# Products of 128 stationary columns in a chunked RWKV recurrence, with one PSUM bank per row side and copies split between ScalarE and VectorE

## The chip, the core and the metric

The kernel runs on one core of one Trainium2 chip. The metric is the device time of the whole program in microseconds, from inputs in HBM to the output in HBM. It is one launch of straight-line code on five engines (TensorE, VectorE, ScalarE, GpSimd, SyncE) that meet through semaphores.

## What is computed

One layer of a diffusion backbone over 2048 latent tokens with 256 context tokens: a token mixer with retention and a bidirectional RWKV-7 scan, then an expert-choice mixture of experts. The change touches only the RWKV scan:

```python
def step(s, xt):                       # per head, 64 x 64 state, every token
    wt, kt, vt, kkt, at = xt[:5]
    sa = jnp.einsum('bhvk,bhk->bhv', s, -kkt)
    s = (s * wt[:, :, None, :] + sa[..., None] * (kkt * at)[:, :, None, :]
         + vt[..., None] * kt[:, :, None, :])
    return s, jnp.einsum('bhvk,bhk->bhv', s, xt[5])
...
for d, f in enumerate((_ident, _flip)):      # both directions, 8 heads
    s_state, o = _rwkv7_scan(zero_rw, f(st_c['w'][d]), f(st_c['k'][d]), f(st_c['v']), f(st_c['kk']), f(st_c['a'][d]), None)
    _, o = _rwkv7_scan(s_state, f(st_l['w'][d]), f(st_l['k'][d]), f(st_l['v']), f(st_l['kk']), f(st_l['a'][d]), f(qu_l['r']))
```

(Cut and joined from the reference.) Everything is float32.

## The kernel before

Stages follow one another: a projection, the scan (`rwkv_chunks`, lines 147 to 876), retention, the mix of heads, the router and the experts. The scan runs the tokens in chunks of 128 per direction, 18 tiles times two directions: 36 slabs, the directions by turns (j % 2). A slab is two halves t of 64 tokens, and eight heads. Inside a half the recurrence is a triangular system, so a slab needs:

- **The inverse.** `pairs` makes the masked products of keys and decayed queries; `couple(l)` and `double(l)` for l from 0 to 4 build the inverse by doubling in f16. VectorE masks what couple made (`levels`, Xb); ScalarE copies what double made (`copies`, Tb and TTb). `errors` and `refine` then sharpen it in f32 (Er, ErH, Gr).
- **The recurrence of a half**, in a chain: `values` (keys' block times v) and `from_state` (decayed keys times the state Hb) add up the right side and, in another part of the bank, the output; ScalarE copies the right side to R (`right_side`); `solve` multiplies by the inverse Gr; ScalarE copies the solution to U (`solved`); `state` makes the new state, which VectorE adds and decays (H, Hb); `outputs` adds U's part of the output, and ScalarE copies it to yo.

Partitions hold two sides of 64 rows, `side(0)` below and `side(1)` above. Each product of 64x64 uses one quarter of the array, and the two sides run beside each other. Half t has a PSUM bank PB[t]: columns 0 to 255 hold the right side and then the solution, 256 to 511 the output. AR holds kkn (k=0) and r (k=1), scaled; BK holds per head four blocks of 64 columns, of which 2 and 3 go into `values`. PB[0] is also RB[1], where the refinement works.

Every engine runs its own list in a fixed order, written out by hand in one loop over the step h. In step h slab h is inverted, slab h+1 is prepared (VectorE's `running`, `centred` D, `exclusive` D2, beta, kappa; ScalarE's exponentials e_bk, e_al, e_rho; GpSimd's products into AR), half 0 of slab h-1 and half 1 of slab h-2 are solved. So pieces of the recurrence stand between the dependent products of the inverse. e_bk waits for D2 (semaphore dd2). SP loads three slabs ahead and stores yo; its waits on `yc` and on the loads' buffers stay.

`pe.matmul(out, stationary, moving)`: the profile's row names the moving operand first and gives stationary rows*columns, then rows x moving columns. One f32 call is two matmul records with two weight loads, one f16 call is one of each.

## Time and profile before

| | us |
|---|---|
| median of 3 runs | 4031.0 (4029.63 to 4033.84) |
| the profiled execution | 4023.1 |
| its span | 4021.3 |
| TensorE matmuls busy in it | 3634.7 (90%) |
| VectorE, ScalarE busy | 2190.9 (54%), 1844.0 (46%) |
| the scan's first and last copy of R | 1297.9, 2131.7 |

The span is the time from the first to the last instruction of the core in one profiled execution; rows carry times from its start. A matmul's end is modelled, and matmuls overlap, so the start of the next is the better measure of pace. "PEld" is the weight load. An idle time "<-issue" is one in which the engine waited for nothing that the profile shows. A group's row in a timeline covers its instructions from the first start to the last end.

### The profile page before, as it was taken

What the parts mean: (1) busy time and instruction counts of PE and PEld (TensorE: products, weight loads), DVE (VectorE), ACT (ScalarE), POOL (GpSimd) and SP (SyncE); (2) the same over time, 40 slices, a digit from 0 to 9 for tenths busy, and PEclk for the clock granted to TensorE, in tenths of its full rate; (3) what the DMA queues carried; (4) which work ended last, traced back from release to release, by engine and by line L of the source; (5) the groups of instructions that cost most, each with busy time, mean ns of one, the idle gap of its engine ahead of it and who ended that gap; (6) DMA issues with size and microseconds to landing.
All of it is one profiled execution on the core that took longest, in us unless ns stands there. A gap on an engine that the chain in (4) does not pass through costs nothing. (4 is left out here: it accounts for less than half of the span.)

```text
span 4021.3 us, 93358 instructions
## 1 busy us (share of the span) xinstructions
PE 3634.7 (90%) x39394; PEld 3022.9 (75%) x39394; DVE 2190.9 (54%) x3518; ACT 1844.0 (46%) x2997; POOL 708.5 (18%) x901
## 2 busy tenths in 40 slices
PE   7999999999997888888787889995799999999993
PEld 6777877878786777777776767784688888888883
DVE  4553453553444666666666864456445445444545
ACT  5653543543443555555555453332344444444443
POOL 1111010010112223232221343100011111111110
PEclk9999999999998999999999999997899999999996
DMA  7566566564556443444414476654466666666667
GB/s 259 187 221 211 166 207 188 153 199 142 172 176 146 100 93 90 91 98 98 111 44 127 152 226 212 200 172 181 145 204 216 219 219 201 217 216 216 205 211 300
DMA packets 443709, 702.90 MB, mean 175 GB/s; under 512 B 182488, under 2 KB 321344, under 8 KB 425808
## 3 DMA queue, kind: packets, MB, share of 16 engines
q1 hardware_dynamic: 409504, 587.23, 47.1%
q0 software_dynamic: 33840, 110.40, 9.0%
q8 instruction: 278, 4.55, 0.5%
q14 instruction: 87, 0.71, 0.1%
HBM read 531.97 MB, written 165.56 MB: 173 GB/s over the span
## 5 line engine op out<-in xcount | busy, mean ns | idle before, releaser
L113 PE MATMUL fro__acc<-fro__hT_hi,fro__wh 128*128 128x512 f32 (+1 forms) x1608 | 629.4, 391 | 12.6 <-DVE fro__hT_lo L2684 8.9
L114 PE MATMUL fro__acc<-fro__hT_hi,fro__wl 128*128 128x512 f32 (+1 forms) x1608 | 614.8, 382 | 0.0
L115 PE MATMUL fro__acc<-fro__hT_lo,fro__wh 128*128 128x512 f32 (+1 forms) x1608 | 614.4, 382 | 0.0
L2014 DVE TENSOR_TENSOR fin__wl<-fin__raw,fin__wh 128x4096 fp32r<-128x4096 f32 x96 | 424.7, 4424 | 317.1 <-ACT fin__wh L1958 317.1
L2690 DVE TENSOR_TENSOR fro__wl<-prj__w,fro__wh 128x1024 fp32r<-128x1024 f32 x201 | 246.3, 1225 | 584.9 <-ACT fro__wh L2427 584.6
L1958 ACT ACTIVATE fin__wh<-fin__raw 128x4096 fp32r<-128x4096 f32 x96 | 348.4, 3629 | 191.2 <-PE exp__acc L115 190.3
L113 PE MATMUL exp__acc<-fin__wh,exp__xh 128*128 128x512 f32 x1024 | 399.9, 390 | 0.7 <-DVE exp__xl L2019 0.7
L115 PE MATMUL exp__acc<-fin__wl,exp__xh 128*128 128x512 f32 x1024 | 398.5, 389 | 0.0
L114 PE MATMUL exp__acc<-fin__wh,exp__xl 128*128 128x512 f32 x1024 | 398.5, 389 | 0.0
L113 PEld LDWEIGHTS fro__acc<-fro__hT_hi,fro__wh 128*128 128x128 f32 x1608 | 305.1, 190 | 87.3 <-issue 31.3
L115 PEld LDWEIGHTS fro__acc<-fro__hT_lo,fro__wh 128*128 128x128 f32 x1608 | 304.9, 190 | 59.2
L114 PEld LDWEIGHTS fro__acc<-fro__hT_hi,fro__wl 128*128 128x128 f32 x1608 | 305.3, 190 | 57.4 <-issue 2.6
L2437 ACT ACTIVATE fro__pool<-fro__acc 128x512 f32<-128x512 f32 (+1 forms) x136 | 79.6, 586 | 433.6 <-PE fro__acc L115 417.8
L566 DVE TENSOR_TENSOR rwc__Xb<-rwc__XB,rwc__level 128x256 f16<-128x256 f32 x360 | 137.1, 418 | 171.6 <-PE rwc__XB L705 169.6
L113 PEld LDWEIGHTS exp__acc<-fin__wh,exp__xh 128*128 128x128 f32 x1024 | 192.3, 188 | 40.4 <-DVE exp__xl L2019 1.1
L115 PEld LDWEIGHTS exp__acc<-fin__wl,exp__xh 128*128 128x128 f32 x1024 | 192.2, 188 | 40.0
L114 PEld LDWEIGHTS exp__acc<-fin__wh,exp__xl 128*128 128x128 f32 x1024 | 192.3, 188 | 39.3
L2427 ACT ACTIVATE fro__wh<-prj__w 128x1024 fp32r<-128x1024 f32 x201 | 212.0, 1055 | 3.5 <-DVE fro__keep L2787 3.5
L113 PE MATMUL exp__acc<-fin__wh,exp__hh 128*128 128x512 f32 x512 | 203.7, 398 | 0.0
L115 PE MATMUL exp__acc<-fin__wl,exp__hh 128*128 128x512 f32 x512 | 200.0, 391 | 0.0
L114 PE MATMUL exp__acc<-fin__wh,exp__hl 128*128 128x512 f32 x512 | 199.7, 390 | 0.0
L372 ACT ACTIVATE rwc__Tb<-rwc__TP 128x256 f16<-128x256 f32 x360 | 121.0, 387 | 69.3 <-PE rwc__TP L715 67.4
(465 smaller groups left out, 7383.3 us busy)
## 6 DMA issues: line engine op xcount, KB each, us to landing
fin__raw<-in_w_x SPq DMA_DIRECT2D x96, 2048.0 KB, 8.4
prj__w<-in_w_z SPq DMA_DIRECT2D x201, 512.0 KB, 4.2
s_zT<-fro__pool SPq DMA_DIRECT2D x128, 256.0 KB, 4.6
fro__wm<-in_w_mod POOLq DMA_DIRECT2D x16, 1024.0 KB, 6.2
mix__gate<-s_zT SPq DMA_DIRECT2D x64, 256.0 KB, 4.2
rwc__ways<-s_ways SPq DMA_DIRECT2D x36, 384.0 KB, 4.5
rwc__ways<-s_ways SPq DMA_DIRECT2D x72, 192.0 KB, 4.8
rwc__both<-s_both SPq DMA_DIRECT2D x36, 384.0 KB, 4.4
```

The costliest lines, as they stand in the source:

```text
L113: pe.matmul(out, sh, mh, start=first, stop=False)
L114: pe.matmul(out, sl, mh, start=False, stop=False)
L115: return pe.matmul(out, sh, ml, start=False, stop=last)
L372: cp = lambda out, in_, n: act.activation(out, in_, ACT.Copy).then_inc(S[n], 1)
L566: tt(Xb[:, g, :, :], h4(XB[g]), level[:, j % 2, l, None, :].to_broadcast([P, GH, HC]), ALU.mult).then_inc(S["xd"], 1)
L1958: act.activation(wh[s][:, :, :], raw[s][:, :, :], ACT.Copy).then_inc(w_hi, 1)
L2014: ve.tensor_tensor(wl[s][:, :, :], raw[s][:, :, :], wh[s][:, :, :], ALU.subtract).then_inc(w_lo, 1)
L2427: act.activation(wh[s % 3][:, :, :], w[s % 3][:, :, :], ACT.Copy).then_inc(split_hi, 1)
L2437: act.activation(zo[i % 3][:, 0:n], acc[t % 3][:, 0:n], fn).then_inc(kept, 1)
L2690: ve.tensor_tensor(wl[s % 3][:, :, :], w[s % 3][:, :, :], wh[s % 3][:, :, :], ALU.subtract).then_inc(split_lo, 1)
```

## The change

`values` and `from_state` take the two blocks of a row side in one product: 64 rows and 128 stationary columns, so the right side comes out on partitions 0 to 63 and the output on 64 to 127. Each row side x writes its own bank QB[x], which holds both halves t in 256 columns each. AR's layout follows. `solve` writes the lower partitions of both banks, `outputs` the upper. ScalarE copies the lower side's R and U, VectorE the upper side's, with semaphores rhd and ud of their own; the output takes two activations. The refinement's second part shares QB[1], so `values` of half 1 waits for Gr of the slab after it. The loops of TensorE, ScalarE and VectorE get another order.

```diff
-        AR = [sb(f"AR{u}", [P, 4, 2, C]) for u in range(B)]
+        AR = [sb(f"AR{u}", [P, 4, 2, 2, HC]) for u in range(B)]
...
-        PB = [room.ps(f"PB{t}", [P, 512]) for t in range(2)]
-        MB, RB = (XB, TP), (EB, PB[0])
+        QB = [room.ps(f"QB{x}", [P, 2, 256]) for x in range(2)]
+        MB, RB = (XB, TP), (EB[:, 0:256], QB[1][:, 0, :])
...
-        part = lambda k, q: slice(256 * k + WD * q, 256 * k + WD * q + WD)
+        part = lambda q: slice(WD * q, WD * q + WD)
...
-                gp.tensor_tensor(AR[j % B][:, :, 0, :], ld[j % LB]["kkn"][:, :, :], e_al[:, :, :], ALU.mult).then_inc(S["al"], 1)
+                gp.tensor_tensor(AR[j % B][:, :, :, 0, :], halves(ld[j % LB]["kkn"]), halves(e_al), ALU.mult).then_inc(S["al"], 1)
...
             def right_side(j, t):
                 act.wait_ge(S[f"rhm{t}"], at(f"rhm{t}", j))
-                cp(R[t][:, :], PB[t][:, 0:256], f"rhc{t}")
+                act.activation(R[t][side(0), :], QB[0][side(0), t, :], ACT.Copy).then_inc(S[f"rhc{t}"], 1)
...
             def solved(j, t):
                 act.wait_ge(S[f"uum{t}"], at(f"uum{t}", j))
-                cp(U[t][:, :], PB[t][:, 0:256], f"uc{t}")
+                act.activation(U[t][side(0), :], QB[0][side(0), t, :], ACT.Copy).then_inc(S[f"uc{t}"], 1)
...
-                cp(yo[t][:, :], PB[t][:, 256:512], f"yc{t}")
+                for x in range(2):
+                    last = act.activation(yo[t][side(x), :], QB[x][side(1), t, :], ACT.Copy)
+                last.then_inc(S[f"yc{t}"], 1)
...
                 n, inverting, prepare = h + 1, h < SLABS, h + 1 < SLABS
-                if exists(h - 2):
-                    right_side(h - 2, 1)
                 if inverting:
                     copies(1, h)
                 if exists(h - 2):
-                    solved(h - 2, 1)
+                    right_side(h - 2, 1)
                 if prepare:
                     scale_bk(n)
+                if exists(h - 2):
+                    solved(h - 2, 1)
                 if inverting:
                     copies(2, h)
+                if exists(h - 2):
+                    outputs(h - 2, 1)
                 if prepare:
                     scale_al(n)
+                if inverting:
+                    copies(3, h)
                 if exists(h - 1):
                     right_side(h - 1, 0)
-                if inverting:
-                    copies(3, h)
                 if prepare:
                     scale_rho(n)
-                if exists(h - 2):
-                    outputs(h - 2, 1)
                 if exists(h - 1):
                     solved(h - 1, 0)
                 if inverting:
@@ -568,7 +571,7 @@
...
+            def right_side(j, t):
+                ve.wait_ge(S[f"rhm{t}"], at(f"rhm{t}", j))
+                ve.tensor_copy(R[t][side(1), :], QB[1][side(0), t, :]).then_inc(S[f"rhd{t}"], 1)
+
+            def solved(j, t):
+                ve.wait_ge(S[f"uum{t}"], at(f"uum{t}", j))
+                ve.tensor_copy(U[t][side(1), :], QB[1][side(0), t, :]).then_inc(S[f"ud{t}"], 1)
...
@@ -607,8 +617,12 @@
                     refine(1, h - 1, 1)
                 if prepare:
                     centred(n)
+                if exists(h - 2):
+                    right_side(h - 2, 1)
                 if inverting:
                     levels(1, h)
+                if exists(h - 2):
+                    solved(h - 2, 1)
                 if prepare:
                     exclusive(n)
                 if inverting:
@@ -617,8 +631,12 @@
                     state(h - 2, 1)
                 if prepare:
                     scaled_removal(n)
+                if exists(h - 1):
+                    right_side(h - 1, 0)
                 if inverting:
                     levels(3, h)
+                if exists(h - 1):
+                    solved(h - 1, 0)
                 if prepare:
                     scaled_keys(n)
...
             def values(j, t):
                 u, s = j % B, turn_of(j, t)
-                if t == 0:
+                if t:
+                    pe.wait_ge(S["yc0"], at("yc0", j))
+                    if exists(j + 1):
+                        pe.wait_ge(S["gd"], at("gd", j + 1))
+                else:
                     pe.wait_ge(S["gd"], at("gd", j))
-                elif j:
-                    pe.wait_ge(S["yc1"], at("yc1", j - 1))
+                    if j:
+                        pe.wait_ge(S["yc1"], at("yc1", j - 1))
...
                 for q in range(4):
-                    for k in range(2):
-                        for x in range(2):
-                            r = side(x)
-                            m = mm(PB[t][r, part(k, q)], BK[u][r, 2 * q + s, 2 + k, :], v_t[u][r, head(q, x ^ s)], start=(q == 0 and k == 0), stop=False,
-                                   skip_group_check=True)
+                    for x in range(2):
+                        r = side(x)
+                        m = mm(QB[x][:, t, part(q)], BK[u][r, 2 * q + s, 2:4, :].rearrange("p k c -> p (k c)"), v_t[u][r, head(q, x ^ s)],
+                               start=q == 0, stop=False, skip_group_check=True)
                 m.then_inc(S[f"vm{t}"], 1)
...
                 for q in range(4):
-                    for k in range(2):
-                        for e in range(2):
-                            m = mm(PB[t][side(e ^ s), part(k, q)], AR[u][side(e), q, k, side(e ^ s)], Hb[j % 2][side(e), q, :], start=False, stop=False,
-                                   skip_group_check=True)
+                    for e in range(2):
+                        m = mm(QB[e ^ s][:, t, part(q)], AR[u][side(e), q, e ^ s, :, :].rearrange("p k c -> p (k c)"), Hb[j % 2][side(e), q, :],
+                               start=False, stop=False, skip_group_check=True)
                 m.then_inc(S[f"rhm{t}"], 1)
...
                 pe.wait_ge(S[f"rhc{t}"], at(f"rhc{t}", j))
+                pe.wait_ge(S[f"rhd{t}"], at(f"rhd{t}", j))
                 pe.wait_ge(S["gd"], at("gd", j))
                 for q in range(4):
                     n = 2 * q + s
-                    for r in map(side, range(2)):
-                        m = mm(PB[t][r, part(0, q)], Gr[j % 2][r, n // GH, n % GH, :], R[t][r, part(0, q)], start=False, stop=True, skip_group_check=True)
+                    for x, r in enumerate(map(side, range(2))):
+                        m = mm(QB[x][side(0), t, part(q)], Gr[j % 2][r, n // GH, n % GH, :], R[t][r, part(q)], start=False, stop=True, skip_group_check=True)
                 m.then_inc(S[f"uum{t}"], 1)
...
                 pe.wait_ge(S[f"uc{t}"], at(f"uc{t}", j))
+                pe.wait_ge(S[f"ud{t}"], at(f"ud{t}", j))
                 for q in range(4):
-                    for r in map(side, range(2)):
-                        m = mm(PB[t][r, part(1, q)], BK[u][r, 2 * q + s, 1, :], U[t][r, part(0, q)], start=False, stop=True, skip_group_check=True)
+                    for x, r in enumerate(map(side, range(2))):
+                        m = mm(QB[x][side(1), t, part(q)], BK[u][r, 2 * q + s, 1, :], U[t][r, part(q)], start=False, stop=True, skip_group_check=True)
...
             inverse_seed(0)
             for h in range(SLABS + 2):
                 p, n, inverting, prepare = h - 1, h + 1, h < SLABS, h + 1 < SLABS
-                if exists(h - 2):
-                    values(h - 2, 1)
-                    from_state(h - 2, 1)
                 if inverting:
                     couple(0, h)
                 if exists(p):
@@ -825,23 +845,25 @@
                 if inverting:
                     double(0, h)
                 if exists(h - 2):
+                    values(h - 2, 1)
+                    from_state(h - 2, 1)
+                if inverting:
+                    couple(1, h)
+                if exists(h - 2):
                     solve(h - 2, 1)
                 if inverting:
-                    couple(1, h)
-                if exists(p):
-                    values(p, 0)
+                    double(1, h)
+                if exists(h - 2):
+                    outputs(h - 2, 1)
                 if inverting:
-                    double(1, h)
+                    couple(2, h)
                 if exists(h - 2) and exists(h):
                     state(h - 2, 1)
                 if inverting:
-                    couple(2, h)
+                    double(2, h)
                 if exists(p):
+                    values(p, 0)
                     from_state(p, 0)
-                if inverting:
-                    double(2, h)
-                if exists(h - 2):
-                    outputs(h - 2, 1)
                 if inverting:
                     couple(3, h)
                 if exists(p):
```

Further, h4 becomes rb4 where RB is read, `state` waits for ud too, and `part` loses an argument there.

On TensorE the head of a step, before:

```order
L681 MATMUL rwc__XB<-rwc__bon,rwc__ones 32x128 x3
L756 MATMUL rwc__PB<-rwc__v_t,rwc__BK 64x64 [waits rwc__yc1]
L756 MATMUL rwc__PB<-rwc__v_t,rwc__BK 64x64 x15
L771 MATMUL rwc__PB<-rwc__Hb,rwc__AR 64x64 [waits rwc__vm1,rwc__hup0]
L771 MATMUL rwc__PB<-rwc__Hb,rwc__AR 64x64 x15
L705 MATMUL rwc__XB<-rwc__Tb,rwc__ATb 64x64 [waits rwc__tbc,rwc__trc,rwc__bonc]
```

and with the change, up to and behind the first double (L733, L738) and from there to outputs (L827):

```order
L699 MATMUL rwc__XB<-rwc__bon,rwc__ones 32x128 x3
L723 MATMUL rwc__XB<-rwc__Tb,rwc__ATb 64x64 [waits rwc__tbc,rwc__trc,rwc__bonc]
...
L738 MATMUL rwc__TTP<-rwc__TTb,rwc__Xb 64x64 x8
L777 MATMUL rwc__QB<-rwc__v_t,rwc__BK 128x64 [waits rwc__gd,rwc__yc0]
L777 MATMUL rwc__QB<-rwc__v_t,rwc__BK 128x64 x7
L791 MATMUL rwc__QB<-rwc__Hb,rwc__AR 128x64 [waits rwc__vm1,rwc__hup0]
L791 MATMUL rwc__QB<-rwc__Hb,rwc__AR 128x64 x7
L723 MATMUL rwc__XB<-rwc__Tb,rwc__ATb 64x64 [waits rwc__tbc]
...
L803 MATMUL rwc__QB<-rwc__R,rwc__Gr 64x64 [waits rwc__gd,rwc__rhd1,rwc__rhc1]
...
L827 MATMUL rwc__QB<-rwc__U,rwc__BK 64x64 [waits rwc__ud1,rwc__uc1]
```

Values and from_state no longer stand between the bonus product and couple; one couple is left between from_state and solve, one double between solve and outputs.

On ScalarE the same stretch of a step (R1, U1 belong to half 1 of slab h-2; e_bk to slab h+1; the copy of U with what stands around it), before:

```order
L372 ACTIVATE rwc__TTb<-rwc__TTP 128x512 [waits rwc__ttm]
L372 ACTIVATE rwc__U1<-rwc__PB1 128x256 [waits rwc__uum1]
L383 ACTIVATE rwc__e_bk<-rwc__D2 128x512 [waits rwc__kappad,rwc__dd2]
L372 ACTIVATE rwc__Tb<-rwc__TP0 128x256 [waits rwc__tm]
L372 ACTIVATE rwc__Tb<-rwc__TP1 128x256 [waits rwc__tm]
```

and with the change:

```order
L373 ACTIVATE rwc__TTb<-rwc__TTP 128x512 [waits rwc__ttm]
L436 ACTIVATE rwc__R1<-rwc__QB0 64x256 [waits rwc__rhm1]
L384 ACTIVATE rwc__e_bk<-rwc__D2 128x512 [waits rwc__kappad,rwc__dd2]
L440 ACTIVATE rwc__U1<-rwc__QB0 64x256 [waits rwc__uum1]
L373 ACTIVATE rwc__Tb<-rwc__TP0 128x256 [waits rwc__tm]
```

The exponential e_bk has moved ahead of the copy of U.

On VectorE (D is `centred`, L537 `exclusive`, with the semaphore dd2), with the change:

```order
L533 TENSOR_TENSOR rwc__D<-rwc__L 128x512 [waits rwc__erho,rwc__eal,rwc__dld,rwc__ebk,rwc__scan]
L596 COPY rwc__R<-rwc__QB 64x256 [waits rwc__rhm1]
L569 TENSOR_TENSOR rwc__Xb<-rwc__XB,rwc__level 128x256 [waits rwc__xm] x2
L600 COPY rwc__U<-rwc__QB 64x256 [waits rwc__uum1]
L537 TENSOR_TENSOR rwc__D<-rwc__D,rwc__ways 128x512 [waits rwc__dd]
L569 TENSOR_TENSOR rwc__Xb<-rwc__XB,rwc__level 128x256 [waits rwc__xm] x2
```

Before, the same rows stand there without the two copies. D2 now stands behind the copy of U.

## Rows read from the trace of the kernel before

**Rows 1.** Busy time by stretch, the middle of the recurrence stage, all engines.

```profile
core 0: us, PE busy (x) PEld busy (x) DVE busy (x) ACT busy (x) POOL busy (x), PEclk, DMA share, GB/s
1300.00:2110.00 810.00, 680.41 (x22994) 613.02 (x22990) 546.29 (x1181) 432.01 (x1114) 241.78 (x401) 0.99 0.40 91
```

**Rows 2.** The copying line of ScalarE, same stretch: ns min/median/max, first and last start.

```profile
L372 ACT ACTIVATE rwc__bo<-rwc__XB x34: 277/278/278, 1310.8 to 2102.3; 128x128 f32<-128x128 f32 x34
```

**Rows 3.** TensorE's waits, same stretch: us in total, times, longest.

```profile
PE rwc__TTP L720 <- issue: 13.8, 18, 1.4
PE rwc__TP L715 <- issue: 12.9, 18, 1.5
...
PE rwc__PB L743 <- DVE rwc__ErH L575: 11.2, 34, 0.4
...
PE rwc__XB L705 <- ACT rwc__Tb L372: 5.6, 18, 0.9
...
PE rwc__TP L691 <- ACT rwc__v_t L372: 4.3, 13, 0.7
...
PE rwc__TP L691 <- issue: 0.2, 1, 0.2
```

**Rows 4.** DMA queues, same stretch: packets, MB, share of 16 engines.

```profile
q8 instruction: 182, 2.98, 1.6%
```

**Rows 5.** TensorE's timeline around a step's head: start, us, instruction, idle before.

```profile
1717.10 0.43 PE L681 MATMUL rwc__XB<-rwc__bon,rwc__ones 128*32 128x128 f32 x8
1717.45 1.15 PE L756 MATMUL rwc__PB<-rwc__v_t,rwc__BK 64*64 64x64 f32 x32
1718.43 1.10 PE L771 MATMUL rwc__PB<-rwc__Hb,rwc__AR 64*64 64x64 f32 x32
1719.37 0.42 PE L705 MATMUL rwc__XB<-rwc__Tb,rwc__ATb 64*64 64x64 f16 x16
1719.62 0.54 PE L743 MATMUL rwc__EB<-rwc__Gr,rwc__Er 64*64 64x64 f32 x12
1721.96 0.33 PE L743 MATMUL rwc__EB<-rwc__Gr,rwc__Er 64*64 64x64 f32 x4 [1.79 <-issue]
...
1722.59 0.29 PE L715 MATMUL rwc__TP<-rwc__Xb,rwc__TTb 64*64 64x64 f16 x8
...
1723.09 0.66 PE L782 MATMUL rwc__PB<-rwc__R,rwc__Gr 64*64 64x64 f32 x16
```

**Rows 6.** TensorE's timeline, a product with 64x128 stationary and one moving column.

```profile
1035.61 0.37 PE L2583 MATMUL fro__rc<-fro__rank_hi,fro__low_lo 64*128 64x1 f32 x4
1035.84 0.36 PE L2583 MATMUL fro__rc<-fro__rank_lo,fro__low_hi 64*128 64x1 f32 x4
...
1036.51 0.36 PE L2583 MATMUL fro__rc<-fro__rank_lo,fro__low_hi 64*128 64x1 f32 x4
```

**Rows 7.** TensorE's timeline in retention, 64x128 stationary and 128 moving columns.

```profile
2284.93 1.06 PE L3238 MATMUL ret__s_p<-ret__qR,ret__kR 64*128 64x128 f32 x16
2285.92 0.66 PE L3273 MATMUL ret__tp<-hold__ident,ret__on 128*128 128x128 f32 x4
```

**Rows 8.** VectorE's timeline, two slabs.

```profile
1700.70 0.68 DVE L534 TENSOR_TENSOR rwc__D<-rwc__D,rwc__ways 128x512 f32<-128x512 f32 x1
...
1715.85 0.29 DVE L575 CAST rwc__ErH<-rwc__Er 128x256 f16<-128x256 f32 x1
...
1717.55 1.21 DVE L522 TENSOR_TENSOR_SCAN rwc__L<-rwc__scanm,rwc__ways 128x512 f32<-128x512 f32 x1
1719.70 0.76 DVE L566 TENSOR_TENSOR rwc__Xb<-rwc__XB,rwc__level 128x256 f16<-128x256 f32 x2 [0.93 <-PE rwc__XB L705]
...
1722.80 0.42 DVE L581 TENSOR_TENSOR rwc__Gr<-rwc__PB,rwc__TTm 128x256 f32<-128x256 f32 x1
```

**Rows 9.** ScalarE's timeline, two slabs.

```profile
1701.42 0.63 ACT L383 ACTIVATE rwc__e_bk<-rwc__D 128x512 f32<-128x512 f32 x1 [1.13 <-DVE rwc__D L534]
1701.95 0.64 ACT L372 ACTIVATE rwc__Tb<-rwc__TP 128x256 f16<-128x256 f32 x2
...
1717.59 0.28 ACT L372 ACTIVATE rwc__bo<-rwc__XB 128x128 f32<-128x128 f32 x1 [0.75 <-PE rwc__XB L681]
1719.58 0.38 ACT L372 ACTIVATE rwc__R<-rwc__PB 128x256 f32<-128x256 f32 x1 [1.72 <-PE rwc__PB L771]
```

More of the change, by code:

```diff
@@ L570, in errors @@
                 ve.wait_ge(S["imt"], at("imt", j, g + 1))
-                tt(Er[:, g, :, :], h4(RB[g]), ImT[:, g, :, :], ALU.add).then_inc(S["ed"], 1)
+                tt(Er[:, g, :, :], rb4(RB[g]), ImT[:, g, :, :], ALU.add).then_inc(S["ed"], 1)
             def rounded_error(j, g):
@@ L580, in refine @@
                     ve.wait_ge(S["tti"], at("tti", j))
-                tt(Gr[j % 2][:, g, :, :], h4(RB[g]), (TTm if r == 1 else TT32)[:, g, :, :], ALU.add).then_inc(S["gd"], 1)
+                tt(Gr[j % 2][:, g, :, :], rb4(RB[g]), (TTm if r == 1 else TT32)[:, g, :, :], ALU.add).then_inc(S["gd"], 1)
             def state(j, t):
@@ L730, in errors @@
                     for z in map(side, range(2)):
[L731 removed]
+                        m = mm(rb4(RB[g])[z, h, :], BK[j % B][z, GH * g + h, 0, :], T32[z, g, h, :], start=True, stop=True)
                 m.then_inc(S["em"], 1)
@@ L742, in refine @@
                     for z in map(side, range(2)):
-                        m = mm(h4(RB[g])[z, h, :], left[z, g, h, :], right[z, g, h, :], start=True, stop=True)
+                        m = mm(rb4(RB[g])[z, h, :], left[z, g, h, :], right[z, g, h, :], start=True, stop=True)
                 m.then_inc(S["gm"], 1)
@@ L794, in state @@
                             r = side(e ^ s)
-                            m = mm(EB[side(e), part(0, q)], key[r, head(q, e)], val[r, part(0, q) if val is U[t] else head(q, e)],
+                            m = mm(EB[side(e), part(q)], key[r, head(q, e)], val[r, part(q) if val is U[t] else head(q, e)],
                                    start=(val is not U[t] and q == 0), stop=val is U[t], skip_group_check=True)
```

9 lines of the change are left out of this document (5 added, 4 removed).

## The prediction

> **What bounds the kernel now.** The change lies in one stage, the chunked RWKV recurrence, which works through 36 slabs. I first read busy time by stretch, to find its limit: between 1300 and 2110 us TensorE's matmuls fill 680 of 810 us, VectorE 546, ScalarE 432, at a granted clock of 0.99, the 2.4 GHz level [rows 1]. The bonus copy that ends each slab stands 34 times from 1310.8 to 2102.3 us, so a slab takes 24.0 us [rows 2]. TensorE is the bound, and what matters is why it ever stands idle. The list of its waits says: 99.7 us of idle in 17 rows (13.8 down to 0.2 us) end in "issue", in other words for nothing that the profile shows; for VectorE's rounded error it waits 11.2 us, for ScalarE's copies of the inverse 5.6 us, for v_t 4.3 us [rows 3]. So nearly every copy is done before TensorE asks for it, and about 2.9 us a slab go to issue. The instruction queue explains that: 182 blocks, 2.98 MB, so 16 KB each, came in this stretch [rows 4], and 22994 matmuls with 22990 weight loads [rows 1] make 253 instructions a block. I read the issue stalls as TensorE waiting for its next block: 0.55 us a block on average, 1.79 us once in the slab shown [rows 5]. The Trainium skill (Runtime: NRT & Kernel Launch, Instruction fetch mechanics) has the same block of 256 instructions but calls the crossing mostly hidden; here it isn't hidden, by the rows above. Taken as that page has it, with an idle that no instruction count or wait changes, the stalls would stay as they are: 4155 us, the third rival below.
>
> **What the change does to TensorE's own work.** Products of values and of state are now 8 calls of 64 rows x 128 columns each instead of 16 calls of 64x64; a call in f32 is two matmul records. Before, one function is 32 records in 0.94 us without its tail, 1718.43 to 1719.37 [rows 5]. Afterwards it is 16 records, in 8 pairs, one record of a pair in each row half. What does such a pair cost? The nearest row is a product of the same stationary form, 64x128 f32, two row halves into two banks, whose moving operand has one column: four records start every 0.22 to 0.23 us, so a pair takes 0.112 us [rows 6]. The same tile with 128 moving columns costs as much: 16 records from 2284.93 to 2285.92, 0.89 us and a switch [rows 7]. The cost does not depend on the moving columns between 1 and 128, so it must be the load of 128 stationary columns, and 64 moving columns lie between. Eight pairs are 0.89 us against 0.94: four functions a slab save **0.2 us**, though half of the records are gone. The other bound is 0.058 us a pair, today's pace of a pair with 64 columns (0.94/16), which would save 1.9 us. The Trainium skill (TensorE: Matmul & The Clock Gate, Back-to-back issue gap) gives an isolated gap of N/2.4 + 2.5 ns by moving columns alone, 29 ns for 64, an estimate that would halve the time; its section LDWEIGHTS, with P/1.2 ns by columns, 107 ns for 128, speaks against this change, and by that rule the trace agrees [rows 6].
>
> Switching the tile's form costs something: the 128x128 record after the 64x128 group starts 0.99 us after its first, 0.10 more than its eight pairs [rows 7]. The new order has four more such switches a slab: **+0.4 us** (bounds 0 and 0.8). Solve and outputs keep 64x64 and their count.
>
> **What it does to the waits.** TensorE takes its instructions in order, so each item is idle time of the bound engine unless work stands ahead of it.
>
> 1. *outputs of the second half, behind VectorE and ScalarE.* On ScalarE, e_bk now stands ahead of the copy of U; e_bk waits for D2, which on VectorE now stands behind the new copy of U, which waits for solve. After solve's last matmul: 0.05 to the copy, 0.32 until VectorE goes on (a copy lies between the cast's 0.29 us and the 0.42 us of an add out of PSUM; I take 0.40, of which 0.08 overlap the next) [rows 8], 0.68 for D2 [rows 8], 0.04 to e_bk (1701.38 to 1701.42), 0.53 until the next copy starts, 0.38 for it [rows 9], 0.05 to TensorE: 2.05 us. In between TensorE has only double, 0.50 us from 1722.59 to 1723.09 [rows 5], of which 0.33 reach beyond the end of solve. **+1.7 us**; behind it on TensorE stands the next couple, and copies of the inverse stand behind U on ScalarE. Half the rows, 64 instead of 128, makes no copy shorter, as far as rows tell: their time goes with elements a row (128 in 0.28 us, 256 in 0.38) [rows 9]. Bounds 1.2 and 2.0.
> 2. *solve behind the copies of R*, for both halves of a slab. After from_state ends: 0.05, 0.38 for the copy, 0.05 make 0.48 [rows 5, 9]. Only one couple stands between, 0.25 us (1719.37 to 1719.62), which ends 0.06 past from_state's tail. **+0.8 us** for two. Before, the copies had a double and more to hide under. Bounds 0.5 and 1.0.
> 3. *couple at the head of the step.* Values and from_state stood between the bonus product and couple, and hid ScalarE's bonus copy. That ends 1717.87, TensorE is free at 1717.45 [rows 5, 9]: **+0.5 us**.
> 4. *double and values.* With couple at 1717.92, two refinements follow until about 1719.1. VectorE's scan ends 1718.76, its two Xb take 0.76, then two sums Gr 0.42 each [rows 8]: Xb ready 1719.5, Gr 1720.2. The second double waits 0.1, and values, which must now wait for Gr of the newer slab because it shares a bank, 0.4: **+0.5 us**.
> 5. *from_state behind values.* Where s is 1 it waits for TensorE's own values; it now follows them directly in both halves, not in one: 0.3 us in half of the slabs, **+0.15 us**.
>
> ScalarE gets two activations more a slab, VectorE four copies of 0.32, 1.3 us on a busy share of 0.67; both stay below TensorE, and cost only through the places above. GpSimd writes the same elements in another order, and its product for a slab is due only at the pairs, us later: nothing. SP's stores wait for yc as before, and their landing has the rest of the slab. The reordering keeps every DMA.
>
> **What is given back.** A wait absorbs the ones behind it: the 5.6 us for Tb are visible idle, with the matmuls' tail more; 0.4 us a slab (bounds 0 and 0.6). And the stalls shrink. A slab issues 128 instructions fewer (64 records and 64 loads), half a block, and the waits give the fetch time. The work per block grows from 3.9 us (810/182 less 0.55) to 24.5/4.8 = 5.1 us. I take 0.2 us a block instead of 0.55, since the waits stand in a few places and the dense stretches keep their stalls: 1.0 us a slab instead of 2.9, rounded **-1.8 us**. Bounds are 0.55 (-0.3) and nothing (-2.9).
>
> **Sum.** -0.2 + 0.4 + 1.7 + 0.8 + 0.5 + 0.5 + 0.15 = 3.85; less 0.4 and 1.8 = 1.65 us a slab; times 36 = **+59 us**. The profiled execution took 4023.1 us (span 4021.3), 0.2% below the median of 4031.0; added to the median: **4090 us**. Stages before and after have not one changed instruction.
>
> **Rivals.**
> - *The load of 128 columns hides* and a pair goes at 0.058 us. For it: today's 0.029 us a record fits 64 moving columns as well as 64 stationary ones. Against it: one moving column is no faster than 128 [rows 6, 7]. It takes 32 x 0.054 = 1.7 us off a slab, of which some 0.3 return as stalls, since the instructions then run denser: 59 - 51 = +8, 4039 us, on the edge of what can be told.
> - *The wait for U doesn't show*, because TensorE comes to outputs late anyway, held by its own Xb or fetch. Against it, only double stands between. It takes 1.7 x 36 = 61 us off: 4029.
> - *The stalls stay.* If their cause isn't the block rate, or the dense stretches keep all, 1.8 x 36 = 65 come on top: 4155; with half of them, 4122.
> - *Faster: the fetch is the real clock.* Place: TensorE's instruction queue. If time goes by blocks, 810/182 = 4.45 us each, and all waits fit into time in which TensorE would stand for a block, 18 blocks fewer are -80 us: 3951. It decides where the new waits stay below the 2.9 us of issue idle a slab; at 3.45 they don't, and the row of waits leaves no more idle to take. A smaller form, waits of 2.0 and all 2.9 of stall gone, gives 4031 - 32 = 3999.
> - *It doesn't do what it says:* the row halves run one after the other, 0.22 us a pair, 32 x 0.11 x 36 = +127 us, 4217. The two records of a pair start together in [rows 6], four in 0.22 us, which is against it.
>
> **Numbers.** Forecast 0.70, load hidden 0.09, U not showing 0.06, stalls staying 0.08, faster 0.05, serial halves 0.02. A difference of 0.2%, 8 us, is about what a measurement of this kernel can tell. The forecast's own bounds, item by item but not all at one end, are 4055 to 4130; taking in part of the neighbours, the range is **4036 to 4135**. The load case lies on the edge (0.04 slower, 0.05 same), the U case spreads over all three (0.02, 0.03, 0.01). So slower: 0.70 + 0.08 + 0.02 + 0.04 + 0.02 = 0.86; same 0.08; faster 0.05 + 0.01 = 0.06.
>
> **What would show it.** Right: the 64x128 products at about 0.112 us a pair; TensorE idle before outputs of the second half, released by ScalarE's U, about 1.5 us visible, 34 times; idle before both solves released by R; issue idle in the stage down from 100 to some 35 us; a slab at 25.7 us. Wrong: pairs at 0.06 us, or issue idle still near 100, or no idle before outputs, each with its price above. If the period falls below 24.0 us, the picture of TensorE paying for every exposed copy is wrong altogether.

## The result, and the profile after

| | before | after |
|---|---|---|
| median of 4 runs, us | 4032.15 | 4142.91 (4131.9 to 4153.06) |
| ratio | | 1.0275, 95% interval 1.0247 to 1.0302 |
| profiled execution / its span, us | 4023.1 / 4021.3 | 4131.9 / 4130.1 |

The change costs 2.75%, 111 us. The direction was forecast, the size was not: 4090 us, range 4036 to 4135. All ratios here are of undisturbed executions; one of the kernel before, on the chip of e5, e6 and e7, took 11317 us at a clock of 0.325 and is left out.

Where the time went, by the same views. First the copying line of ScalarE that ends each slab, in the kernel after (count, ns min/median/max, first and last start):

```profile
L373 ACT ACTIVATE rwc__bo<-rwc__XB x36: 277/277/278, 1263.0 to 2197.9; 128x128 f32<-128x128 f32 x36
```

35 slab periods take 934.9 us; before, the same 36 copies start from 1268.2 to 2102.3, 834.1 us. That is +100.8 of the 108.8 us between the two profiled executions. Another +15.6 lies directly behind, in the drain of the last two slabs: from the last bonus copy to the first product of retention it is 50.9 us (to 2248.8) instead of 35.3 (to 2137.6). The stage starts 5.2 us earlier, as it does in four of the other runs (e4, e5, e7, e10) and not in the rest, and retention and what follows take 2.4 us less; neither is put down to the change.

Busy time in the stretch of [rows 1], after:

```profile
core 0: us, PE busy (x) PEld busy (x) DVE busy (x) ACT busy (x) POOL busy (x), PEclk, DMA share, GB/s
1300.00:2110.00 810.00, 672.58 (x18341) 604.72 (x18340) 536.40 (x1166) 418.46 (x1047) 202.22 (x357) 0.89 0.38 86
```

TensorE is busy about as long as before. The stretch has a fifth fewer matmuls, for two reasons: a slab has 616 matmul records instead of 680, and only some 30 slabs fall into the stretch instead of 34. The number to see is the one that the prediction read once and never used again: the granted clock, 0.99 before, is 0.89 now. TensorE's waits in that stretch (us in total, times, longest), to set beside [rows 3]:

```profile
PE rwc__QB L827 <- ACT rwc__U L440: 44.8, 30, 1.7
PE rwc__TP L709 <- DVE rwc__TTb L564: 18.6, 23, 1.0
PE rwc__XB L723 <- ACT rwc__bo L373: 11.9, 30, 0.4
PE rwc__QB L803 <- ACT rwc__R L436: 10.9, 46, 0.6
PE rwc__QB L761 <- DVE rwc__ErH L578: 10.4, 30, 0.3
PE rwc__QB L777 <- DVE rwc__Gr L584: 6.9, 22, 0.3
PE rwc__XB L723 <- ACT rwc__Tb L373: 6.4, 27, 0.2
```

The wait of outputs for U is there as forecast, 1.5 us each time, 30 times in this stretch. Issue idle fell from 99.6 to 21.7 us (3.0 to 0.7 a slab), and the instruction queue brought 146 blocks instead of the 182 of [rows 4] (4.8 a slab instead of 5.4). The TTb row (inverse_seed, L709) takes the place of the 4.3 us for v_t at the same line before, L691 in [rows 3]; that it would grow was not forecast.

Now the same slabs one by one, from bonus copy to bonus copy (TensorE busy, PEclk, DMA share, GB/s):

```profile
1634.66:1665.78 31.12, 26.64 (x616) 0.73 0.33 73
1665.78:1693.08 27.30, 22.70 (x616) 0.87 0.38 85
1693.08:1719.90 26.82, 22.53 (x616) 0.87 0.36 82
1719.90:1744.62 24.72, 20.27 (x616) 1.00 0.38 83
1744.62:1771.03 26.41, 22.21 (x616) 0.94 0.36 84
1771.03:1795.76 24.73, 20.69 (x616) 1.00 0.39 90
```

Each slab has 616 matmul records, and its length follows its clock: 24.7 us at 1.00, 26.4 at 0.94, 27 at 0.87, 31 at 0.73. Of the 34 slabs from the second bonus copy on, 8 stand at 1.00 and take 24.72 to 25.08 us, in the mean 24.80; all 34 have a mean of 26.96. By itself this does not say which is the cause, since a slab that waits longer could also lose clock by it; the fillers below decide that. Within a slab the clock falls to the lower of its two levels, 1.2 GHz, and comes back:

```profile
1693.10:1698.60 5.50, 4.57 (x128) 1.00 0.60 126
1698.60:1705.40 6.80, 5.42 (x144) 0.50 0.05 13
1705.40:1719.90 14.50, 12.54 (x348) 1.00 0.41 97
1744.60:1753.20 8.60, 5.92 (x180) 1.00 0.53 115
1753.20:1756.60 3.40, 3.40 (x98) 0.50 0.10 24
1756.60:1771.00 14.40, 12.89 (x344) 1.00 0.33 80
```

TensorE's timeline at the second fall shows what it had done before:

```profile
1753.07 0.70 PE L827 MATMUL rwc__QB<-rwc__U,rwc__BK 64*64 64x64 f32 x10 [1.67 <-ACT rwc__U L440]
```

It had stood still for 1.67 us, and at 1753.2 it was at half speed for the next 3.4. In the first case no pause in the 5.5 us before the fall was longer than 0.4 us; values and from_state with their 128-column products (1695.7 to 1698.1) had just run. That TensorE's clock follows how busy it was is also what the Trainium skill says (TensorE: Matmul & The Clock Gate, Part 1); the trace agrees for the second fall, which stands right behind a wait.

The drain is the place where the clock is lowest: it was 0.99 there before, and in the kernel after it stays at the lower level from 2217.5 us to the end. Before, after, the end of the drain after, and, for later, the drain of e3:

```profile
2102.30:2137.60 35.30, 26.70 (x929) 0.99 0.09 24
```
```profile
2197.90:2248.80 50.90, 37.57 (x768) 0.69 0.07 17
2217.50:2248.80 31.30, 21.18 (x248) 0.50 0.06 14
```
```profile
2159.50:2198.85 39.35, 24.62 (x928) 0.99 0.09 22
```

One group of values takes 1.11 us at the higher level and 1.98 at the lower:

```profile
2206.67 1.11 PE L777 MATMUL rwc__QB<-rwc__v_t,rwc__BK 64*128 64x64 f32 x16
2219.30 1.98 PE L777 MATMUL rwc__QB<-rwc__v_t,rwc__BK 64*128 64x64 f32 x16 [0.61 <-DVE rwc__Gr L584]
```

### The profile page after: what moved, and what is told of

It is laid out like the page before. It is cut to its first block and busy times, and to the rows that moved or that the text cites. A ratio compares the mean times of both kernels' runs of the same rounds, so it can differ in the third digit from the quotient of the medians.

```text
span 4130.1 us, 89142 instructions
## 1 busy us (share of the span) xinstructions
PE 3714.7 (90%) x37090; PEld 3096.2 (75%) x37090; DVE 2252.8 (55%) x3662; ACT 1885.6 (46%) x3069; POOL 696.6 (17%) x901
```

## The experiments

The theory after this reading: three things were added to TensorE's path (waits, the form of the products, fewer stalls in return), and on top of them a term that the prediction did not have, the clock. All ratios are set against the kernel before on the same chip; the clock and the issue idle are those of 1300 to 2110 us.

| run | ratio to before (95%) | median us | clock | issue idle us |
|---|---|---|---|---|
| after | 1.0275 (1.0247, 1.0302) | 4142.9 | 0.89 | 21.7 |
| e1_fill | 1.0230 (1.0207, 1.0252) | 4119.0 | 0.91 | 19.3 |
| e2_u_first | 1.0223 (1.0197, 1.0250) | 4109.1 | 0.93 | 21.5 |
| e3_64cols | 1.0168 (1.0149, 1.0186) | 4090.2 | 0.93 | 66.4 |
| e4_bk_late | 1.0132 (1.0107, 1.0157) | 4072.2 | 0.94 | 29.7 |
| e5_64_bk_late | 1.0122 (1.0094, 1.0150) | 4073.5 | 0.95 | 105.8 |
| e6_fill3 | 1.0237 (1.0212, 1.0263) | 4118.9 | 0.94 | 24.7 |
| e7_before_bk_first | 0.9999 (0.9982, 1.0016) | 4022.1 | 0.99 | 77.0 |
| e9_fill_full | 1.0191 (1.0174, 1.0208) | 4099.5 | 0.99 | 18.0 |
| e10_act_both | 1.0308 (1.0286, 1.0330) | 4143.6 | 0.91 | 25.2 |
| e11_bk_fill2 | 1.0090 (1.0074, 1.0107) | 4060.4 | 0.98 | 21.6 |
| e12_order64 | 1.0069 (1.0049, 1.0089) | 4053.0 | 0.95 | 95.0 |
| e13_order64_fill | 1.0097 (1.0077, 1.0118) | 4064.1 | 0.97 | 76.0 |

### Is it the clock? e1_fill, e6_fill3, e9_fill_full

A direct test: give TensorE work that nobody needs while it waits. If only the wait mattered, that could gain nothing. One line of the diff is broken for its length.

```diff
             def outputs(j, t):
                 u, s = j % B, turn_of(j, t)
+                if t and j + 2 < SLABS:
+                    for i in range(12):
+                        for z in map(side, range(2)):
+                            mm(XB[0][z, 0:256].rearrange("p (h c) -> p h c", h=4), ident2b[z, :],
+                               ident2b[z, None, :].to_broadcast([HC, 4, HC]), start=True, stop=True)
                 pe.wait_ge(S[f"uc{t}"], at(f"uc{t}", j))
```

> The kernel after, with 24 products that nothing reads (stationary 64x64, 256 moving columns, into XB[0]) put at the head of TensorE's outputs(h-2, 1), ahead of its wait for U, so that TensorE works while it would have stood still. Theory C (the granted clock: TensorE's new waits let it fall again and again, and that costs 69 us of the stage, 35 slab periods of 934.9 us against 35 x 24.73): the added work takes the 1.35 us of the wait and no more, the wait row of U (49.8 us) nearly goes, the clock of the stage rises from 0.88 to 0.95 or more, and the time falls to 4075 to 4105. Rival W (the waits themselves are the loss, at whatever clock): the products change nothing, since U comes when it comes: 4135 to 4155. Rival D (the added products come on top): 4170 to 4200.

Measured: 4119.0, above the range of theory C and below that of W, clock 0.91 (18 us less than after, by the ratios, with intervals that overlap a little). The filler took 1.5 us. The next expectation says that it overshot the wait by 0.5; the trace does not bear that out. In 23 of the 34 filled slabs outputs started 0.05 us behind the end of ScalarE's copy of U, in 10 others 0.13 to 0.22 us, and once 0.8: some 2 us in all. What happened is that the clock now fell at another place. In the kernel after, 9 of the 25 falls between 1300 us and the last bonus copy start 7.9 to 9.2 us behind a bonus copy, that is in the wait for U or right behind it; in e1 none does, and 12 of 26 start in the first 0.8 us of the slab, where one had. The time at the lower level went from 177 to 143 us. The direction is that of theory C, but most of the loss is still there, and by itself this run decides little. The next had shorter filler at three places:

> The kernel after, with products that nothing reads put into three places where TensorE stood still: 18 ahead of the wait for U, 8 ahead of inverse_seed's wait for TTb, 4 ahead of each half of refine(0), all of 64x64 stationary and 256 moving columns in f16. In the first try 24 at the U wait took 1.5 us and overshot it by 0.5, and the clock still fell behind the head of the slab. Theory C (the clock falls because of these thin stretches, and its falls are a large part of the loss): clock of the stage 0.95 or more, time 4080 to 4110 although TensorE computes nothing sooner. Rival (the clock follows something else, or costs little): clock below 0.93, time 4130 to 4170.

Measured: 4118.9, between both ranges again, and a clock of 0.94, just short of what theory C wanted. Its waits say why:

```profile
PE rwc__QB L707 <- ACT rwc__v_t L373: 23.5, 29, 1.0
...
PE rwc__QB L837 <- ACT rwc__U L440: 10.4, 16, 0.7
```

L707 is the filler in inverse_seed, which stood behind the wait for v_t and ahead of that for TTb. So where the kernel after shows "<- DVE rwc__TTb", ScalarE's copy of v_t had as a rule ended only shortly before, and the filler came on top of that wait. The third try changed two things at once, so their shares can't be told: it put the filler in front of both waits, and it used the whole array, at the same three places:

```diff
             def inverse_seed(j):
+                for i in range(5 if 1 < j < SLABS else 0):
+                    mm(QB[0][:, 1, :].rearrange("p (h c) -> p h c", h=4), firstb[:, :, :].rearrange("p a c -> p (a c)"),
+                       ident2b[:, None, :].to_broadcast([P, 4, HC]), start=True, stop=True)
                 pe.wait_ge(S["m1d"], at("m1d", j))
```

(and the same call 3 times ahead of each half of refine(0), and 9 times into XB[0] ahead of the U wait.)

> As the run with three fillers, but each filler is a product of 128x128 stationary and 256 moving columns in f16 (9 ahead of the U wait, 5 ahead of inverse_seed's waits, 3 ahead of each half of refine(0)), so the whole array works, and the filler at inverse_seed stands ahead of the wait for v_t too, where the last run showed the wait of 26.5 us to lie. Nothing of it is read. Theory C (the granted clock is the term that the forecast lacked, some 45 to 50 us): the clock of the stage comes back to 0.97 or more, slabs come every 24.7 to 25.2 us throughout, time 4085 to 4105. Rival (falls of the clock cost no more than 15 us here): the clock may rise, the time stays at 4120 or above.

Measured: 4099.5 at a clock of 0.99, as theory C has it; only the slabs were a little longer than it said, most of them 25.1 to 25.9 us. TensorE's busy time in the stretch, and in three of its slabs:

```profile
1300.00:2110.00 810.00, 726.14 (x19930) 0.99 0.39 90
...
1389.55:1414.66 25.11, 22.75 (x636) 1.00 0.42 99
1414.66:1440.54 25.88, 23.03 (x636) 1.00 0.35 84
...
1543.00:1568.11 25.11, 22.88 (x636) 1.00 0.42 94
```

The clock is back at 0.99, and 20 more matmul records a slab make the kernel faster by 0.84% (1.0275 against 1.0191), 34 us; by the profiled executions the 35 periods shrink from 934.9 to 895.7 us, 39 us. The filler has a price of its own, though: the shortest slab at full clock takes 25.11 us with it and 24.72 without, some 13 us for 34 slabs. So the falls of the clock cost the kernel after an estimated 52 us in its 35 periods, and that is the missing term. It is an estimate with wide bounds. 39 us is what was gained with the filler taken as free. If every slab of the kernel after took the 24.80 us of its eight at full clock, 67 us would go, but some of that is issue idle and not clock.

The drain has hardly any filler in e9; it stands at 0.75 and takes 49.3 us. In e3 below it is at 0.99 and takes 39.35, with 64-column products. Ten groups at 0.42 us more each (1.11 against 0.69 us) would make that 43.5 with 128 columns, so an estimated 7 of the 15.6 us in the drain are the clock too; the groups that ran at half speed there, summed by their two durations, give 9.

### What else is in the stage? e2, e4, e7: one line on ScalarE

e2_u_first swaps two calls of the kernel after:

```diff
                 if inverting:
                     copies(1, h)
                 if exists(h - 2):
                     right_side(h - 2, 1)
-                if prepare:
-                    scale_bk(n)
                 if exists(h - 2):
                     solved(h - 2, 1)
+                if prepare:
+                    scale_bk(n)
                 if inverting:
                     copies(2, h)
```

e4_bk_late puts scale_bk(n) behind copies(2, h) as well, and e7_before_bk_first makes the opposite swap in the kernel before.

> The kernel after, with ScalarE's copy of U(h-2, 1) ahead of e_bk instead of behind it. Theory: the wait row of U (49.8 us) goes, but copies(2, h) stays behind e_bk, so a wait of couple(2, h) on ScalarE's Tb comes in its place (some 25 to 35 us); the waits add up to a little less, the clock stays near 0.89, and the time falls by 10 to 25 us, to 4118 to 4133. Rival (U was the only thing behind e_bk that mattered): the 49.8 us go and the clock comes back, 4060 to 4090.

> The kernel after, with ScalarE's e_bk behind both the copy of U(h-2, 1) and copies(2, h). Theory: the wait of TensorE for U goes and nothing takes its place (e_bk is not wanted before the next slab's pairs), about 45 us at the clock as it is, and with it the falls of the clock that follow the wait, up to 30 us more: 4060 to 4100, clock of the stage 0.93 or more. Rival (e_bk is then late for VectorE's scaled keys and what hangs on it): 4120 to 4160, with a wait of pairs for BK in the list.

e2: 4109.1, below the expected 4118 to 4133, on a chip where the kernel before takes 4026 us instead of 4032. By the ratios, 0.0052 x 4025, it is 21 us less than after, inside the 10 to 25 expected, though the two intervals just touch. The clock was expected to stay and went from 0.89 to 0.93. The U row is gone from the list, and in its place stands the copy that is now queued behind e_bk:

```profile
PE rwc__XB L723 <- ACT rwc__Tb L373: 28.9, 61, 0.9
```

e4: 4072.2, in the range, 58 us less than after by the ratios; no row of U or Tb above 7 us, and the clock at 0.94. One ScalarE instruction in the wrong place was worth 1.4% of the whole kernel: up to 45 us of waits, and falls of the clock with them. In the kernel before the same instruction costs nothing:

> The kernel before with one line moved: ScalarE's e_bk ahead of its copy of U(h-2, 1), as in the change; banks, products and every other order are those of before. There U is wanted later, by state(h-2, 1), so a part of the wait stays hidden. Theory: a wait of state for U of 0.3 to 0.8 us for each slab, some falls of the clock with it, +10 to +45 us over before. Rival (in the order of before the cover is long enough): within 5 us of before, clock 0.97.

```profile
PE rwc__EB L795 <- ACT rwc__U L372: 14.4, 22, 0.8
...
PE rwc__TP L715 <- issue: 10.5, 15, 1.4
```

Ratio 0.9999. The wait appears, 14.4 us of it, and issue idle falls from 99.6 to 77.0 in exchange. Here both readings had a part in it: the wait of the theory, the time of the rival. The new wait was free here: it stood where TensorE would have waited for instructions, and the clock stayed up (0.99).

### Were 128 columns a good form? e3, e5

e3_64cols keeps banks, copies and order, and issues the products as four of 64x64, one for each quarter of the array:

```diff
                 for q in range(4):
-                    for x in range(2):
-                        r = side(x)
-                        m = mm(QB[x][:, t, part(q)], BK[u][r, 2 * q + s, 2:4, :].rearrange("p k c -> p (k c)"), v_t[u][r, head(q, x ^ s)],
+                    for k in range(2):
+                        for x in range(2):
+                            r = side(x)
+                            m = mm(QB[x][side(k), t, part(q)], BK[u][r, 2 * q + s, 2 + k, :], v_t[u][r, head(q, x ^ s)],
```

(from_state likewise.)

> The kernel after (its banks, its copies, its order), with the products of values and from_state of 64 stationary columns again, 64 more for each slab. Theory: this alone brings the instruction count back to that of before, so the issue idle of TensorE comes back in part (from 22.5 us to 50 to 80), and the products themselves take the same engine time or 0.1 us more for each group (pairs of 128 columns took 1.11 us for 16, 0.50 for 16 of double): 4145 to 4185. Rival (the form of 128 columns is slow in itself and is what costs the time): 4100 to 4125.

Both missed: 4090.2, 43 us better than after by the ratios (0.0107 x 4025). The groups by shape in 1300 to 2110 us (count, busy us, mean ns): first the kernel before, then after, then e3.

```profile
L756 PE MATMUL rwc__PB<-rwc__v_t,rwc__BK 64*64 64x64 f32 x2176 | 80.9, 222 | 6.4 <-issue 6.4
```
```profile
L777 PE MATMUL rwc__QB<-rwc__v_t,rwc__BK 64*128 64x64 f32 x960 | 72.4, 291 | 12.0 <-DVE rwc__Gr L584 6.9 <-issue 5.1
```
```profile
L778 PE MATMUL rwc__QB<-rwc__v_t,rwc__BK 64*64 64x64 f32 x1984 | 49.6, 233 | 13.0 <-issue 6.6 <-DVE rwc__Gr L584 6.3
```

One values is 32 records before (1.19 us busy each, 80.9/68), 16 after (1.21, 72.4/60) and 32 in e3 (0.80, 49.6/62). These means mix slabs at both levels of the clock. At the higher level one group takes 1.15 us before (1717.45 in [rows 5]), 1.11 after (the row at 2206.67 above), and in e3

```profile
2161.83 0.69 PE L778 MATMUL rwc__QB<-rwc__v_t,rwc__BK 64*64 64x64 f32 x32
```

So the price of a 128-column product was forecast well, and it was the wrong comparison. A group of 128-column calls takes as long as twice as many of 64 columns in two quarters; over four quarters the 64-column calls run beside each other. The old layout put both blocks of a row half into the same quarter, and could use only two; the new banks open the other two, and the 128-column form gives that back. The Trainium skill states this concurrency (TensorE: Matmul & The Clock Gate, Part 3: Packing small matmuls); the trace agrees, 0.69 against 1.11 us. Four such groups a slab would be 60 us in 36 slabs; 43 were gained, with the clock at 0.93 instead of 0.89 and issue idle at 66.4 us instead of 21.7.

> Both edits at once: products of 64 stationary columns in the new banks, and ScalarE's e_bk behind the copy of U(h-2, 1) and copies(2, h). In the run with 64 columns alone a group of values took 0.48 us from its first to its last start where the 128 columns took 0.84, and the time fell by about 50 us; with e_bk alone moved it fell by about 65. Theory (two separate losses, of the array's time in the 128-column products and of the wait for U, with the clock following both): they add up but for some new issue idle, 4020 to 4050, near the kernel before. Rival (both only cure the same idle before the outputs): 4065 to 4085.

Measured: 4073.5, the range of the rival, though not by its mechanism. The two gains don't add. The U wait is gone, and issue idle has come:

```profile
PE rwc__QB L778 <- issue: 15.0, 15, 2.0
PE rwc__TP L733 <- issue: 14.2, 16, 1.8
...
PE rwc__TTP L738 <- issue: 12.4, 14, 2.7
PE rwc__XB L723 <- issue: 12.2, 12, 3.3
PE rwc__EB L819 <- issue: 11.7, 13, 3.6
```

105.8 us against 29.7 in e4. With 128 fewer instructions a slab the kernel after had bought itself out of these stalls; with 64-column products they are back, and the denser work left TensorE standing for instructions. That it waits there for its next block is still a reading, as in the prediction: no run set the rate of the blocks by itself.

### Is the split between two engines worth anything? e10

```diff
             def right_side(j, t):
                 act.wait_ge(S[f"rhm{t}"], at(f"rhm{t}", j))
-                act.activation(R[t][side(0), :], QB[0][side(0), t, :], ACT.Copy).then_inc(S[f"rhc{t}"], 1)
+                for x in range(2):
+                    last = act.activation(R[t][side(x), :], QB[x][side(0), t, :], ACT.Copy)
+                last.then_inc(S[f"rhc{t}"], 1)
```

(solved likewise; VectorE's two functions and their waits are gone.)

> The kernel after with both halves of R and U copied by ScalarE, one after the other, and none by VectorE. Theory: a second copy of 0.38 us stands on the path of solve (twice a slab) and of outputs and state; the waits for R and U grow by 0.3 us in each of the three or four places, 30 to 45 us, and a little clock with them: 4160 to 4200. Rival (VectorE's half is what TensorE waits for, and taking it away frees it): 4110 to 4140.

Measured: 4143.6, ratio 1.0308 against 1.0275, so some 13 us more than after, with intervals that overlap a little; it lies between the expected range and that of the rival. Its waits:

```profile
PE rwc__QB L791 <- ACT rwc__R L437: 27.4, 60, 0.5
PE rwc__XB L712 <- ACT rwc__Tb L373: 21.2, 30, 0.8
PE rwc__QB L813 <- ACT rwc__U L443: 20.3, 30, 1.0
```

The waits for R grow from 10.9 to 27.4 and for Tb from 6.4 to 21.2, as a second copy on one engine should make them. But the wait for U shrinks from 44.8 to 20.3: VectorE no longer stands waiting for U ahead of D2, so e_bk comes earlier (it starts 0.35 us behind the last product of solve, 1.44 in the kernel after; medians of 36). The split gives with one hand what it takes with the other.

### Towards a better version: e11, e12, e13

> The kernel with e_bk behind copies(2, h) (4072 us, clock of the stage 0.93), with the fillers of full width at inverse_seed (5) and ahead of the halves of refine(0) (3 each), which nothing reads. Theory C: added work at the two thin places of the slab's end brings the clock to 0.97 and the time down to 4045 to 4065 although 11 products are added to each slab. Rival (the fillers only add time): 4075 to 4100.

Measured: 4060.4, clock 0.98, theory C again: on a base without the U wait, 11 useless products a slab gain 0.42% (1.0132 to 1.0090). e12 takes the 64-column products and a new order:

```
TensorE, calls of a step (guards left out):
  couple(0) refine(1, p, 0) refine(1, p, 1) double(0) values(h-2, 1) from_state(h-2, 1) couple(1) solve(h-2, 1)
  double(1) outputs(h-2, 1) couple(2) state(h-2, 1) values(p, 0) double(2) couple(3) from_state(p, 0) double(3)
  couple(4) solve(p, 0) double(4) pairs(n, 0) state(p, 0) pairs(n, 1) outputs(p, 0) errors(0) turn(0) turn(1)
  turn(2) errors(1) refine(0, 0) inverse_seed bonus refine(0, 1)
ScalarE: scale_bk, scale_al, scale_rho behind outputs(h-2, 1); right_side(h-1, 0) behind copies(3),
  solved(h-1, 0) behind copies(4)
```

> A new order on ScalarE, VectorE and TensorE for the new banks with products of 64 columns, looked for so that no copy stands late: e_bk, e_al and e_rho follow the output copy, from_state, solve, state and outputs of half 0 each come one step of the inverse later, and refine(0) is split around inverse_seed. Theory: less waiting than in the kernel with both edits (4073 us, 1.012 of before), by 20 to 25 us in about equal issue idle, and with it fewer falls of the clock: 4020 to 4055, ratio to before 1.000 to 1.008. Rival (with 64 columns TensorE then waits for instructions what it no longer waits for copies): 4065 to 4080.

> The same order with fillers that nothing reads, of 128x128 stationary and 256 moving columns: 4 at inverse_seed, 2 ahead of each half of refine(0). If falls of the clock are left in the run without them, they go: 5 to 15 us less than that run. If the run without them stands at a clock of 0.98 already or is bound by issue idle, the fillers cost 0 to 15 us.

e12: 4053.0, the best that the new banks gave, and still 0.7% above the kernel before. The time lies in the expected range, but against e5 the waits for copies fell only from 66.6 to 59.9 us and the clock stayed at 0.95; issue idle fell by 11 us. Its issue idle is 95.0 us, about as much as in the kernel before, but the waits for VectorE and ScalarE come to 59.9 us where they were 22.2, and the clock is 0.95. e13: the clock goes up by 0.02, the filler costs more than that brings, +11 us; VectorE's Xb is now what TensorE waits for most, 35.5 us in 57 times. No version beat the kernel before.

## Why the prediction was wrong

By its own steps:

- **The array's own work, -0.2 a slab: right.** At the higher level of the clock a group takes 1.11 us instead of 1.15; the one moving column of [rows 6] did give the pace of the 64x128 form. Rival "load hides": out. The price of switching the tile's form, +0.4, was not taken apart by any run. What was not asked is what the new banks would give with 64 columns (e3).
- **1, outputs behind U, 1.5 us visible: right.** 44.8 us in 30 times, and e4 shows that order alone makes it.
- **2 to 5: too high in sum.** R 10.9 us in 46 waits, bonus copy 11.9 in 30, Gr 6.9 in 22: 1.0 us a slab, where 1.95 were forecast. Item 5 did not come: from_state's wait for values is 2.7 us in 17 times, before and after.
- **The 0.4 a slab given back for Tb: wrong.** Its wait did not go into another; it is 6.4 us in 27 times, where it was 5.6 in 18.
- **The slab without the clock: near, partly by luck.** A slab was put at 25.7 us. The filled run, at full clock and with what stalls are left, has 25.80 in the mean of 34 (877.05/34), less 0.39 for the filler 25.4; before it was 23.93 in the same count (813.8/34). The waits of 2 to 5 were forecast too high by about as much as the missed TTb wait and the Tb term were too low.
- **The stalls, -1.8: a little short.** Issue idle went from 99.6 to 21.7 us, not to 35, 2.2 us a slab. That waits and issue idle replace each other is seen twice more (e5, e7).
- **The wait in inverse_seed, 18.6 us where it was 4.3: missed.** "Both stay below TensorE, and cost only through the places above" was wrong there: with the issue idle ahead of it gone, TensorE comes earlier to a chain (VectorE's BK, ScalarE's ATb, v_t) that is no faster than before. The runs without filler fit this: at 66 to 106 us of issue idle this wait is 4 to 13 us (before, e7, e3, e5), at 22 to 30 it is 15 to 21 (after, e2, e4, e10). With +0.5 us a slab it grew most after the one for U. Its parts were not taken apart.
- **The drain, +15.6: missed.** The sum took 36 equal slabs; the last two have no other slab's work to hide a lengthened chain, and TensorE, with more pauses, ran its last 31 us at half speed. An estimated 7 to 9 us of it are the clock, the rest the chain.
- **The step that failed is one that isn't there: the clock.** "At a granted clock of 0.99, the 2.4 GHz level" was read from [rows 1] and kept for the sum. The forecast moved idle time from many short stalls into a few pauses of 1.5 us, and never asked what the clock would do. It fell to 0.89, and to 0.69 in the drain, and cost an estimated 52 us in the periods and 7 to 9 behind them.

The account of the 108.8 us: 52 clock inside the 35 periods; 49 waits, switches and products less stalls there (58 were forecast for as many); 15.6 drain, of it 7 to 9 clock; the remaining -7.6 outside the change. Only the sums are measured, the share of the clock is the estimate above. Without the clock the rest would have made some 4031 + 49 + 7 = 4087, against 4090, by errors of both signs. The rival "the stalls stay" gives 4155 and looks close; it is refuted by the issue row. It would have been right by accident.

What stays open: which of TensorE's thin places, the U wait, the 128-column groups or the slab's end, makes how many of the falls, and what the clock costs within the bounds above. Filling only one (e1) moved them to another; removing one (e2, e4) took part of them away. 15 of the 25 falls of the kernel after start ahead of the wait for U, 4.9 to 6.7 us behind the bonus copy, and no run took these apart. And a filler does not always pay: on e12 (e13) it brought the clock up and cost 11 us.

## What to carry to other kernels

Where TensorE is the bound, read the granted clock before and ask what it will be after: pauses of less than 2 us were paid twice here, once as waits and, by the estimate, about as much again as work at half speed. A cheap test is work that nobody reads, put into the pause: if the kernel gets faster by it, the clock was part of the loss; if it doesn't, nothing is said, since the filler has a price too (e13). And before narrow products are merged into wide ones to save instructions, ask whether the narrow ones could run in different quarters of the array at the same time.

## What the runs showed of the hardware

- A f32 call with 128 stationary columns takes as long as two with 64 in the same quarter (1.11 and 1.15 us for one values at the higher clock, tails included); the same values as 64x64 calls over four quarters take 0.69 us.
- The clock fell from 2.4 to 1.2 GHz 24 times between 1300 and 2130 us, in stretches of 3.4 to 17.1 us, in a stage where TensorE's longest wait was 2.1 us. Slabs with equal work took 24.7 to 31.8 us, in step with it.
- Products that nobody reads, put into TensorE's pauses, raised the clock from 0.89 to 0.99 and made the kernel 34 us faster (e9); on e12's order they raised it from 0.95 to 0.97 and made it 11 us slower (e13).
- Copies of 64x256 f32 take ScalarE 0.36 to 0.38 us, where R with 128x256 took 0.38, and VectorE 0.42.
- Issue idle and waits for VectorE and ScalarE replace each other: 99.6 and 22.2 us in the kernel before, 77.0 and 39.5 with one late copy more (e7), at the same total time.
